# Pooling head and router of an expert-choice MoE encoder: rows spread by the tensor engine, constants loaded later, projection ahead of pooling, router on unnormed rows

## The chip, the cores and the metric

One core of one Trainium2 chip. The metric is the device time of one execution in microseconds (us), the median of several. The engines are PE (matmul), DVE (vector), ACT (scalar), POOL (GpSimd) and SP (which only issues DMAs here). Each engine runs its own list of instructions in order; they are tied together by semaphores, which one engine raises and another waits for.

## The reference, cut to what matters

2048 rows of x and 16 meta rows ahead of them make T = 2064 rows of D = 1024. Depth is 1, so there is one pooling mixer and one mixture of experts.

```python
h = concat([meta, x])                      # (2064, 1024)
u = rmsnorm(h, norm_mix)
for g, win in enumerate((2, 4, 8, 16)):    # 256 columns each
    p[g] = window_mean(u[g], win) - u[g]
h = h + concat(p[g] @ pool_w[g]) * pool_scale
u = rmsnorm(h, norm_ffn)
aff = softmax(u @ router_w)                # 16 experts
g, idx = top_k(aff.T, 258)                 # each expert picks 258 rows
ys = (silu(u[idx] @ w_gate) * (u[idx] @ w_up)) @ w_down * g
h = h.at[idx].add(ys)
out = rmsnorm(h, norm_final)[16:]
```

## The kernel before

It has three stages in one program. **Stage 1** (the head and a loop over 19 tiles, up to about 150 us) takes tiles of 128 rows that advance by 112 (eight rows of halo on either side). **Stage 2** (to about 214 us) turns the logits into affinities, finds each expert's threshold by a search in octal digits and makes the list of the first expert. **Stage 3** runs the 16 experts with split fp32 weights (a rounded high part and a rest, three products), and the final norm. The change touches stage 1 and the first lines of stage 2.

What happens to tile t in stage 1, with the engine and the line of the profile in brackets:

- SP loads `h_in` (L521; four buffers, so tile t+4 is asked for when tile t is `mixed`).
- `square_in`: ACT squares and sums each row (L839) and takes the root (L827).
- `make_band`: DVE inverts it (L1077) and scales the pooling matrix with it into `band` (L1081). There are three kinds of pooling matrix: kind 0 for the first tile, 1 for the middle ones, 2 for the last.
- PE pools: 8 fp32 matmuls of 128 columns, 16 passes in the profile, into banks 0 and 1 (L1505, `bank<-band,h_in`).
- ACT rounds the result to `pooled_hi` (L855); DVE takes the rest, `pooled_lo` (L1099).
- PE projects: 24 matmuls of 256 columns with `pw_hi` and `pw_lo`, into banks 2 and 3.
- DVE adds `h_in` and writes `h_mid` (L1118, semaphore `mixed`); SP stores it to `h_acc` (L563).
- ACT squares `h_mid` (L864) and takes the root; DVE inverts it and writes `u_out` = h_mid x inverse x norm_ffn (L1109, semaphore `normed`); SP stores it to `u_rows` (L567).
- PE turns `u_out` (8 transposes, L1510) into banks 4 and 5; ACT copies them to `u_t` (L874).
- PE forms the logits with `rw_wide` (16 passes of 32 weight columns), DVE copies them to `partial` (L1095), and one more matmul with the constant `fold` puts the tile's 16 logits per row into bank 6 (semaphore `routed`).

The work is software pipelined. "Step i" of an engine holds, in this order, on PE: pooling of tile i+1, logits of tile i-3, projection of tile i, fold of tile i-3, turning of tile i-2. On DVE: band of i+2, partial of i-3, pooled_lo of i+1, u_out of i-1, h_mid of i. On ACT: pooled_hi of i+1, square_in of i+2 (in the written-out steps before the loop `square_in` comes first), square of h_mid i-1, u_t of i-2. Steps -1 to 2 are written out (`FIRST = 3`), then a loop of 3 turns with 4 steps each, then the last steps are written out, up to step NT + 2 = 21. The steps above NT are the tail, where PE turns rows first.

Before step 0 the weights of the projection are made: `scale_weights(i)` on DVE multiplies one half of `pool_w` by norm_mix (a column per partition, `nmix`, turned by PE from `nmix_rows`) and by pool_scale (`pscale`, the row copied to all 128 partitions by DMA), 4 instructions for a half (L1134); ACT rounds the half to `pw_hi` (L880); DVE takes the rest, `pw_lo` (L1143). SP issues every load of the head in one list: the meta rows, tile 0, kind 0, the identity, the norm row, tile 1, kind 1, `pscale`, both halves of `pool_w`, tile 2, `nffn`, `rw`, kind 2, tile 3, then `chunk_quad`, `far`, `reset`, the other constants and `nfin`. The last eight that count for `loaded_c` are waited for together by POOL, DVE and PE.

After step 21 DVE waits for all 19 folds and starts the softmax: the maximum (L1174), the subtraction (L1175), and ACT the exponential (L891).

## Time and profile before

| | us |
|---|---|
| median of 3 runs | 2455.67 |
| lowest and highest run | 2455.53, 2458.54 |
| the profiled execution's own time | 2459.78 |
| its span from first to last instruction | 2457.9 |
| PE busy in it | 2386.1 (97%) |
| DVE, ACT, POOL busy | 1865.9, 1204.1, 844.8 |
| mean granted PE clock | 0.984 of full |

The profile is of one execution. Its own time lies 4.1 us above the median of the timed runs, and its span lacks 1.9 us of it, which is start and end outside the first and last instruction. A timeline row gives the start, the length (for a group, from first start to last end), the engine, the line, the operation with output and inputs, the count, and in brackets how long the engine had been idle before it and what released it. A PE matmul in fp32 appears as two passes.

### The profile page before, as it was taken

How to read it: one execution, taken by the hardware profiler on the slowest of the kernel's cores; microseconds unless marked ns; L12 is line 12 of the kernel's file. 1: busy time of each engine (PE TensorE's matmuls, PEld its weight loads, DVE VectorE, ACT ScalarE, POOL GpSimd, SP SyncE). 2: the span in 40 equal slices, each digit the busy share in tenths (PEclk: the TensorE clock that was granted, in tenths of full speed). 3: DMA queues.
4: the chain of work that ended last, by engine and by line, in shares of the span. 5: the costliest groups of instructions: out<-in, count | busy, mean ns of one | idle time of the engine just before them, and what ended most of it. 6: DMA issues, size and time to landing. Idle time of an engine off the chain costs nothing.

```text
span 2457.9 us, 48606 instructions
## 1 busy us (share of the span) xinstructions
PE 2386.1 (97%) x17338; PEld 2228.5 (91%) x17338; DVE 1865.9 (76%) x2259; ACT 1204.1 (49%) x1938; POOL 844.8 (34%) x1013
## 2 busy tenths in 40 slices
PE   7958999999999999999999999999999999999997
PEld 7947989898999989899998989899998989899996
DVE  5666786869787786968788686968778686968765
ACT  5754444444544444454444444454444444454564
POOL 0001525234251524334251524335152533425111
PEclk9978999999999999999999999999999999999998
DMA  7764648486775858586774858586674948576594
GB/s 236 215 195 131 186 133 257 150 243 184 210 201 157 228 144 252 158 238 173 207 213 141 242 141 249 157 238 188 184 216 136 250 143 250 170 228 199 161 335 171
DMA packets 345810, 486.11 MB, mean 198 GB/s; under 512 B 23117, under 2 KB 294997, under 8 KB 345778
## 3 DMA queue, kind: packets, MB, share of 16 engines
q1 hardware_dynamic: 318370, 433.82, 59.2%
q0 software_dynamic: 23232, 36.67, 7.0%
q10 hardware_dynamic: 4176, 15.21, 1.6%
q8 instruction: 18, 0.29, 0.0%
q14 instruction: 14, 0.11, 0.0%
HBM read 443.27 MB, written 46.31 MB: 199 GB/s over the span
## 4 chain that ended last, share of the span: by engine, by line
PE 87%; issue 3%; DVE 1%; POOL 1%; ACT 1%; DMA 0%; DVEq 0%; POOLq 0%; ACTq 0%
PE bank L1505 86%; PE bank L1510 1%; ACT marks_a L913 0%; POOL fin L788 0%; DMA x_rows<-u_rows,idx 0%; DVE w_lo L1345 0%; POOL h_rows L796 0%; DVE h_rows L1466 0%; POOL fin L784 0%; POOL out L817 0%; DVE x_lo L1350 0%; DVE key_t L1226 0%; DVE y_rows L1457 0%; DVE marks_v L1200 0%; DVE flag L1207 0%
## 5 line engine op out<-in xcount | busy, mean ns | idle before, releaser
L1505 PE MATMUL bank<-x_lo,w_hi 128*128 128x258 f32 x4096 | 1157.6, 283 | 0.0
L1505 PE MATMUL bank<-x_hi,w_hi 128*128 128x258 f32 x4096 | 1156.5, 282 | 0.8 <-DVE w_lo L1345 0.7
L1505 PE MATMUL bank<-x_hi,w_lo 128*128 128x258 f32 x4096 | 1155.9, 282 | 0.0
L1345 DVE TENSOR_TENSOR w_lo<-raw,w_hi 128x1024 fp32r<-128x1024 f32 x584 | 713.8, 1223 | 114.0 <-ACT w_hi L935 109.7
L1505 PEld LDWEIGHTS bank<-x_hi,w_hi 128*128 128x128 f32 x4096 | 776.1, 189 | 14.7 <-issue 13.0
L1505 PEld LDWEIGHTS bank<-x_hi,w_lo 128*128 128x128 f32 x4096 | 777.6, 190 | 0.0
L1505 PEld LDWEIGHTS bank<-x_lo,w_hi 128*128 128x128 f32 x4096 | 776.9, 190 | 0.6
L935 ACT ACTIVATE w_hi<-raw 128x1024 fp32r<-128x1024 f32 x581 | 612.2, 1054 | 312.0 <-PE bank L1505 295.2
L671 POOL TENSOR_TENSOR carrier<-carrier 128x1 f32<-128x1 f32 x360 | 115.3, 320 | 1125.7 <-ACT y_rows L986 454.8
L716 POOL DMA_INDIRECT list_rows<-pair_now,slot_now x285 | 410.1, 1439 | 137.1 <-issue 137.1
L1371 DVE SCALAR_TENSOR_TENSOR acc_left<-raw,hid_left,acc_left 128x1024 f32<-128x1024 f32 x330 | 422.5, 1280 | 0.0
L1404 DVE TENSOR_TENSOR hid<-silu,bank 128x258 f32<-128x258 f32 x256 | 108.1, 422 | 329.4 <-PE bank L1505 329.4
L1505 PE MATMUL bank<-w_hi,hid_hi 128*128 128x512 f32 x960 | 304.5, 398 | 0.0
L1505 PE MATMUL bank<-w_lo,hid_hi 128*128 128x512 f32 x960 | 299.7, 393 | 0.0
L1505 PE MATMUL bank<-w_hi,hid_lo 128*128 128x512 f32 x960 | 299.2, 393 | 0.0
L1003 ACT ACTIVATE hid_left<-hid 128x2 f32<-128x2 f32 x244 | 49.7, 204 | 435.2 <-DVE hid L1404 435.2
L1345 DVE TENSOR_TENSOR w_lo<-raw_more,w_hi 128x1024 fp32r<-128x1024 f32 x184 | 224.8, 1222 | 40.2 <-ACT w_hi L935 38.4
L935 ACT ACTIVATE w_hi<-raw_more 128x1024 fp32r<-128x1024 f32 x184 | 193.7, 1053 | 101.8 <-PE bank L1505 101.8
L998 ACT ACTIVATE silu<-bank 128x258 f32<-128x258 f32 x256 | 99.0, 387 | 280.9 <-PE bank L1505 280.9
L1505 PEld LDWEIGHTS bank<-w_hi,hid_lo 128*128 128x128 f32 x960 | 180.6, 188 | 41.4
L1505 PEld LDWEIGHTS bank<-w_lo,hid_hi 128*128 128x128 f32 x960 | 180.4, 188 | 41.2
L1505 PEld LDWEIGHTS bank<-w_hi,hid_hi 128*128 128x128 f32 x960 | 175.1, 188 | 35.5
(209 smaller groups left out, 1887.9 us busy)
## 6 DMA issues: line engine op xcount, KB each, us to landing
raw<-in_moe_w_down SPq DMA_DIRECT2D x98, 1024.0 KB
raw<-in_moe_w_gate SPq DMA_DIRECT2D x97, 1024.0 KB
raw<-in_moe_w_up SPq DMA_DIRECT2D x97, 1024.0 KB
raw_more<-in_moe_w_gate SPq DMA_DIRECT2D x31, 1024.0 KB
raw_more<-in_moe_w_up SPq DMA_DIRECT2D x31, 1024.0 KB, 8.5
raw_more<-in_moe_w_down SPq DMA_DIRECT2D x30, 1024.0 KB, 6.5
h_in<-in_x SPq DMA_DIRECT2D x18, 512.0 KB, 5.6
h_acc<-h_mid SPq DMA_DIRECT2D x17, 448.0 KB, 4.9
```

The costliest lines, as they stand in the source:

```text
L671: nc.gpsimd.tensor_tensor(carrier[:, 0:1], carrier[:, 1:2], carrier[:, 1:2], ALU.mult)\
L716: pool.indirect_dma_start(list_rows, bass.IndirectOffsetOnAxis(ap=slot_now[:, c:c + 1], axis=0), pair_now[:, c, :], None, bounds_check=CAP ...
L935: nc.scalar.activation(w_hi[:, a % 4], split_view(a, last), ACT.Copy).then_inc(split_hi, 1)
L998: nc.scalar.activation(silu[:, fc], bank[:, q % 4, 0:CAP], ACT.Silu)\
L1003: nc.scalar.activation(hid_left[:, 4 * b + fc], hid[:, fc % 2, 256:CAP], ACT.Copy)\
L1345: nc.vector.tensor_tensor(w_lo[:, a % 4], split_view(a, last), w_hi[:, a % 4].bitcast(f32), ALU.subtract).then_inc(split_lo, 1)
L1371: nc.vector.scalar_tensor_tensor(out=acc_left[:, t], in0=down_row_view(k), scalar=by, in1=acc_left[:, t], op0=ALU.mult, op1=ALU.add)\
L1404: nc.vector.tensor_tensor(hid[:, fc % 2], silu[:, fc], bank[:, q % 4, 0:CAP], ALU.mult).then_inc(hid_done, 1)
L1505: return nc.tensor.matmul(dst, lhs, rhs, start=start, stop=stop)
L1510: return nc.tensor.matmul(dst, src, ident[0:n, 0:n], is_transpose=True, start=True, stop=True)
```

## The change

- `pscale` and `nffn` are no longer loaded as a row copied to 128 partitions (512 KB each). ACT issues four small loads at its start, ahead of its table load: the 8 rows of norm_mix and of norm_ffn into `nmix_rows` (now 16 rows), and the row of pool_scale and of norm_ffn, each into one partition of `h_mid`. PE spreads each with two matmuls of 512 columns, weights `ones` of one row (`spread_row`): pool_scale into banks 2 and 3, where `scale_weights` reads it, norm_ffn into banks 4 and 5, from where ACT copies it to `nffn`.
- PE runs `square_ones(6)` (6 matmuls of 128 columns that nothing reads) before the first spread and `square_ones(12)` after the second.
- SP loads `pool_w` before tile 1 and kind 1. Kind 2, `chunk_quad`, `far`, `reset` and `nfin` (five loads) are issued by `load_late`, after `tile_out(0)` and `tile_out(1)`, ahead of `tile_out(2)`.
- In DVE's head, tile 1's band moves behind the making of the weights. On ACT, `square_in` of tile 1 moves behind both `pw_hi`, and in step 0 `square_in` of tile 2 now comes after `pooled_hi` of tile 1 (`early` is 0 < i0 < FIRST).
- On PE, in step 0 the pooling of tile 1 comes after the projection of tile 0 (`pool_rows`).
- The router works on `h_mid`: PE turns `h_mid` instead of `u_out`, a step earlier (tile i-1 at the end of step i, logits and fold of i-2 in step i). norm_ffn goes into `rw_wide` (POOL), and the inverse root mean square is applied to all logits at once in stage 2: `rms2` keeps all 19 columns, a reciprocal and one more multiplication by `inv_all` come ahead of the maximum. PE's and DVE's last step is NT + 1 instead of NT + 2, ACT's NT instead of NT + 1.

The diff, cut:

```diff
@@ SP, the head's loads
             load_kind(0, loaded_kind0)
-            sp.dma_start(ident[:], ...).then_inc(loaded_nmix, 16)
-            sp.dma_start(nmix_rows[:], norm_mix[0].rearrange("(k p) -> k p", p=P)).then_inc(loaded_nmix, 16)
-            load_tile(1, 1)
-            load_kind(1, loaded_kind1)
-            sp.dma_start(pscale[:], pool_scale[0].partition_broadcast(P)).then_inc(loaded_pw[0], 16)
+            sp.dma_start(ident[:], ...).then_inc(loaded_ident, 16)
             for i in range(2):
                 ...
                 sp.dma_start(pw[:, half], pool_w_v[:, half]).then_inc(loaded_pw[i], 16)
+            load_tile(1, 1)
+            load_kind(1, loaded_kind1)
             load_tile(2, 2)
-            sp.dma_start(nffn[:], norm_ffn[0].partition_broadcast(P)).then_inc(loaded_c, 16)
             sp.dma_start(rw[:], ...).then_inc(loaded_c, 16)
-            load_kind(2, loaded_c)
             load_tile(3, 3)
-            (chunk_quad, far, reset: three loads)
             sp.dma_start(cst[:, POOL_COLS:], consts[:, POOL_COLS:]).then_inc(loaded_c, 16)
-            sp.dma_start(nfin[:], norm_final.partition_broadcast(P)).then_inc(loaded_c, 16)
+            def load_late():
+                (kind 2, chunk_quad, far, reset, nfin: five loads, each .then_inc(loaded_late, 16))
...
             for i in range(FIRST - 1):
                 tile_out(i, 0, load_tile)
+            load_late()
@@ POOL
-            nc.gpsimd.tensor_copy(rw_wide[:, :, 0:NE], rw[:]).then_inc(rw_widened, 1)
+            pool.wait_ge(nmix_out, 1)
+            nffn_across = nmix[:, KD:2 * KD].unsqueeze(2).broadcast_to([P, KD, NE])
+            nc.gpsimd.tensor_tensor(rw_wide[:, :, 0:NE], rw[:], nffn_across, ALU.mult).then_inc(rw_widened, 1)
@@ ACT
+            for i, rows in enumerate((norm_mix, norm_ffn)):
+                nc.scalar.dma_start(nmix_rows[KD * i:KD * (i + 1), :], rows[0].rearrange("(k p) -> k p", p=P))\
+                  .then_inc(loaded_nmix, 16)
+            for i, row in enumerate((pool_scale, norm_ffn)):
+                nc.scalar.dma_start(h_mid[0:1, i, :], row).then_inc(loaded_rows[i], 16)
             nc.scalar.preload_act_table(ACT.Sqrt)
...
-                early = isinstance(j, int) and i0 < FIRST
+                early = isinstance(j, int) and 0 < i0 < FIRST
...
             square_in(-1, 0, 1)
-            step(-1, 0)
+            act.wait_ge(pooled, 1)
+            nc.scalar.activation(pooled_hi[:, 0, :], two_banks(0), ACT.Copy).then_inc(pooled_hi_done, 1)
             for k in range(0, KD, 4):
                 act.wait_ge(weights_scaled, k + 4)
                 nc.scalar.activation(pw_hi[:, k:k + 4], pw[:, k:k + 4], ACT.Copy).then_inc(weights_hi, 1)
+            square_in(0, 0, 1)
+            act.wait_ge(nffn_spread, 1)
+            nc.scalar.activation(nffn[:], two_banks(4), ACT.Copy).then_inc(nffn_out, 1)
@@ DVE, the head
-            dve.wait_ge(loaded_kind1, 16)
-            make_band(0, 0, 1)
+            dve.wait_ge(scale_spread, 1)
...
             scale_weights(0)
             step(-1, 0, banded_before=True)
             scale_weights(1)
-            (pw_lo of both halves)
+            split_weights(0)
+            split_weights(1)
+            dve.wait_ge(loaded_kind1, 16)
+            make_band(0, 0, 1)
@@ DVE, the start of stage 2
+            dve.wait_ge(rooted2, NT)
+            link(nc.vector.reciprocal(inv_all[:], rms2[:]))
             dve.wait_ge(routed, NT)
-            link(nc.vector.tensor_reduce(peak[:], logits, AX.X, ALU.max))
-            nc.vector.tensor_tensor(lg[:], logits, over_experts(peak[:]), ALU.subtract).then_inc(shifted, 1)
+            link(nc.vector.tensor_tensor(lg[:], logits, over_experts(inv_all[:]), ALU.mult))
+            link(nc.vector.tensor_reduce(peak[:], lg[:], AX.X, ALU.max))
+            nc.vector.tensor_tensor(lg[:], lg[:], over_experts(peak[:]), ALU.subtract).then_inc(shifted, 1)
@@ PE
             def turn_rows(i0, j):
-                s = (i0 - 2) % 2
-                pe.wait_ge(normed, upto(i0, j, -2))
+                s = (i0 - 1) % 2
+                pe.wait_ge(mixed, upto(i0, j, -1))
                 ...
-                                      u_out[:, s, k * P:(k + 1) * P])
+                                      h_mid[:, s, k * P:(k + 1) * P])
...
+            def square_ones(times):
+                for _ in range(times):
+                    mm(bank[:, 6, 0:P], ones[:], ones[:], True, True)
+
+            def spread_row(i, done):
+                pe.wait_ge(loaded_rows[i], 16)
+                for half in range(2):
+                    last = mm(bank[:, 2 + 2 * i + half, :], ones[0:1, :],
+                              h_mid[0:1, i, half * 512:half * 512 + 512], True, True)
+                last.then_inc(done, 1)
+
+            pe.wait_ge(setup_p, 1)
+            square_ones(6)
+            spread_row(0, scale_spread)
+            pe.wait_ge(loaded_ident, 16)
             pe.wait_ge(loaded_nmix, 32)
-            turn_block(bank[:, 7, 0:KD], nmix_rows[:]).then_inc(nmix_turned, 1)
+            turn_block(bank[:, 7, 0:2 * KD], nmix_rows[:]).then_inc(nmix_turned, 1)
             for i in range(-1, FIRST):
                 ...
                 step(i, 0)
+                if i == -1:
+                    spread_row(1, nffn_spread)
+                    square_ones(12)
...
-            for i in range(FIRST + BODY * TURNS, NT + 3):
+            for i in range(FIRST + BODY * TURNS, NT + 2):
                 step(i, 0)
```

## Rows read from the trace of the kernel before

**Rows 1.** The page, section 1: span, then busy time of each engine.
```profile
span 2457.9 us, 48606 instructions
PE 2386.1 (97%) x17338; PEld 2228.5 (91%) x17338; DVE 1865.9 (76%) x2259; ACT 1204.1 (49%) x1938; POOL 844.8 (34%) x1013
```
**Rows 2.** The chain that ended last, one piece: start, length, what.
```profile
333.12 129.15 PE bank L1505 x932
```
**Rows 3.** Timeline of all engines, 0 to 20 us: start, length, engine, line, operation.
```profile
6.75 0.49 DVE L1081 TENSOR_SCALAR band<-cst,inv 128x512 f32<-128x512 f32 x1
7.29 3.47 PE L1505 MATMUL bank<-band,h_in 128*128 128x128 f32 x16 [1.10 <-DVE band L1081]
10.80 1.02 ACT L855 ACTIVATE pooled_hi<-bank 128x1024 fp32r<-128x1024 f32 x1 [2.10 <-PE bank L1505]
11.71 1.67 DVE L1134 SCALAR_TENSOR_TENSOR pw<-pw,nmix,pscale 128x256 f32<-128x256 f32 x4 [2.19 <-DMA pw<-in_pool_w]
12.84 2.03 SPq L546 DMA_DIRECT2D chunk_quad<-in_consts  x1
13.30 1.22 DVE L1099 TENSOR_TENSOR pooled_lo<-bank,pooled_hi 128x1024 fp32r<-128x1024 f32 x1
14.66 3.75 PE L1505 MATMUL bank<-band,h_in 128*128 128x128 f32 x16 [3.90 <-DVE pooled_lo L1099]
16.01 2.43 DVE L1143 TENSOR_TENSOR pw_lo<-pw,pw_hi 128x1024 fp32r<-128x1024 f32 x2
17.09 1.04 ACT L839 ACTIVATE squares<-h_in 128x1024 f32<-128x1024 f32 x1
18.25 0.29 ACT L827 ACTIVATE rms<-ss,eps 128x1 f32<-128x1 f32 x1
18.50 0.58 PE L1505 MATMUL bank<-pw_hi,pooled_hi 128*128 128x256 f32 x1
```
**Rows 4.** Slices of 1 us: busy PE, PEld, DVE, ACT, POOL; granted clock; DMA share; GB/s.
```profile
13.00:14.00 1.00, 0.00 (x0) 0.00 (x0) 1.00 (x2) 0.59 (x1) 0.00 (x0) 0.85 1.01 410
20.00:21.00 1.00, 1.00 (x8) 1.00 (x8) 0.73 (x1) 0.97 (x3) 0.00 (x0) 0.74 0.72 276
```
**Rows 5.** Timeline of all engines, 20 to 45 us.
```profile
24.18 0.38 SPq L521 DMA_DIRECT2D h_in<-in_x  x1
30.88 1.06 ACT L839 ACTIVATE squares<-h_in 128x1024 f32<-128x1024 f32 x1 [4.19 <-DMA h_in<-in_x]
38.05 0.38 SPq L521 DMA_DIRECT2D h_in<-in_x  x1
44.51 1.05 ACT L839 ACTIVATE squares<-h_in 128x1024 f32<-128x1024 f32 x1
```
**Rows 6.** Timeline of PE alone, 36.5 to 49 us.
```profile
37.34 0.38 PE L1505 MATMUL bank<-pw_hi,pooled_hi 128*128 128x256 f32 x1
40.57 1.07 PE L1510 MATMUL bank<-ident,u_out 128*128 128x128 f32 x8
41.48 2.00 PE L1505 MATMUL bank<-band,h_in 128*128 128x128 f32 x16
48.18 0.90 PE L1505 MATMUL bank<-band,h_in 128*128 128x128 f32 x6
```
**Rows 7.** DMA issues, 0 to 60 us: count, KB each, median us to landing.
```profile
h_in<-in_x SPq DMA_DIRECT2D x9, 512.0 KB, 5.8
nfin<-in_norm_final SPq DMA_DIRECT2D x1, 512.0 KB, 6.5
```
**Rows 8.** Timeline of all engines, 139 to 152 us.
```profile
139.71 1.23 DVE L1118 TENSOR_TENSOR h_mid<-bank,h_in 128x1024 f32<-128x1024 f32 x1 [0.86 <-PE bank L1505]
144.45 1.02 ACT L874 ACTIVATE u_t<-bank 128x1024 f32<-128x1024 f32 x1
150.23 0.61 PE L1505 MATMUL bank<-cst,partial 128*128 128x16 f32 x2 [0.41 <-DVE partial L1095]
151.46 0.47 DVE L1175 TENSOR_TENSOR lg<-bank,peak 128x304 f32<-128x304 f32 x1
```

More of the change, by code:

```diff
@@ L187, in encoder_kernel @@
         far = sb("far", [P, 1], f32)
+        rms2 = sb("rms2", [P, NT], f32)
+        inv_all = sb("inv_all", [P, NT], f32)
         listed = sb("listed", [P, 3, 5], f32)
@@ L509, in upto, with column @@
             return i0 + a + 1 + BODY * j
+        def column(i0, j, a):
+            return slice(i0 + a, i0 + a + 1) if isinstance(j, int) else ds(i0 + a + BODY * j, 1)
         def turn(i0, j, a, ring):
@@ L1134, in scale_weights, with split_weights @@
                     nc.vector.scalar_tensor_tensor(out=pw[:, k, :], in0=pw[:, k, :], scalar=nmix[:, k:k + 1],
-                                                   in1=pscale[:, g * GD:(g + 1) * GD], op0=ALU.mult,
+                                                   in1=two_banks(2)[:, g * GD:(g + 1) * GD], op0=ALU.mult,
                                                    op1=ALU.mult).then_inc(weights_scaled, 1)
+            def split_weights(i):
+                half = slice(4 * i, 4 * i + 4)
+                dve.wait_ge(weights_hi, i + 1)
+                nc.vector.tensor_tensor(pw_lo[:, half], pw[:, half], pw_hi[:, half].bitcast(f32),
+                                        ALU.subtract).then_inc(pw_split, 1)
             scale_weights(0)
@@ L1527, in step @@
                 tail = isinstance(j, int) and i0 >= NT
[L1528 removed]
+                if tail and here(-1):
                     turn_rows(i0, j)
[L1530 to L1543 removed]
+                if here(1) and not (isinstance(j, int) and i0 == 0):
+                    pool_rows(i0, j)
+                if here(-2):
+                    pe.wait_ge(turned_out, upto(i0, j, -2))
+                    s = (i0 - 2) % 2
+                    if i0 == 2:
                         pe.wait_ge(rw_widened, 2)
[L1545 to L1546 removed]
+                    if upto(i0, 0, -4) > 0:
+                        pe.wait_ge(part_out, upto(i0, j, -4))
                     for k in range(KD):
```

124 lines of the change are left out of this document (64 added, 60 removed).

## The prediction

> **What bounds the kernel now.** I read the page first: PE is busy 97% of a span of 2457.9 us [rows 1]. The chain of waits shows where: from 214 us on it is PE in long pieces, such as 129.15 us without a break in one expert [rows 2]. No line of the experts changes, so nothing is to be had or lost there, and everything from the softmax to 214 us is a chain of short waits that the change moves as a whole but for one multiplication. So the question is only at what time the softmax starts: the last fold ends at 150.84 and the subtraction at 151.93 [rows 8]. I then read the timeline up to 152 us, and the slices of 1 us for the clock. The loop over tiles is bound by PE too: pooling of one tile at 41.48, of the next at 48.18, 6.70 us a step with the turning, projection and logits between them and no idle time [rows 6]. What does not lie on PE's time there is hidden, and what stops PE there is lost for good. So two places carry the sum: the head, until PE runs without breaks, and the tail, from the last `h_mid` on.
>
> **The change part by part.**
>
> The head before, for comparison: pooling of tile 0 takes 7.29 to 10.76, the weights arrive at 11.71, `pw_lo` is ready at 18.44, the projection starts at 18.50, and pooling of tile 1 has filled the wait (14.66 to 18.41) [rows 3]. The first projection that starts in a full step is tile 3's, at 37.34 [rows 6]. That is the mark against which I walk through the head after. All steps below are start plus duration, in the order of each engine's list.
>
> Loads. Two copies of 512 KB leave the head, and `pool_w` goes ahead of tile 1 and kind 1: some 1.3 MB instead of 2.6 MB lie ahead of its first half's end. The half landed at 11.71 [rows 3]; at the roughly 0.3 MB per us that the DMA engines move in full slices (410 and 276 GB/s [rows 4]) it lands near 7.4, the second half near 9. The row of pool_scale is issued by ACT as its third load, at some 1.6 us; no row shows such a load, so it lands between 3.5 and 6; I take 4.2, since no large transfer is ahead of it on its queue.
>
> PE's new work. 8 fp32 matmuls of 128 columns (1024 columns) took 3.47 us at the start [rows 3] and 2.00 us in the loop [rows 6]: the pace of the 1.2 and of the 2.4 GHz level. (The slices call the clock 1.00 before 13 us, but the pace is that of the low level.) `square_ones(6)` is 768 columns, 2.6 us at the low level, 1.1 to 3.7. `spread_row` is 1024 columns with one row of weights. I charge it like a pooling, 3.47 us at the low level: 4.2 to 7.7. This holds the queue: the turn of the norm rows and the pooling of tile 0, which started at 7.29, wait behind it, and so does `scale_weights(0)`, which needs the spread. The rule that speaks against this edit is in the Trainium skill, "TensorE: Matmul & The Clock Gate", section "Why this matters for your kernels": a matmul with few rows of weights takes the same time as one with 128. By it the spread costs what I charge; were it cheaper in proportion to its rows, pooling of tile 0 could start at 7.3 and the sum would be 0.6 us lower. No row here shows a one-row matmul of this width.
>
> The clock. A busy PE got the high level within slice 20:21, about 6 us after it had begun at 14.66, and had lost it in slice 13:14, about 3 us after its work had ended at 10.76 [rows 3, 4]. Busy from 1.1 on, with half a us of gap, it would have the high level near 7.1. So I let the pooling of tile 0 run at the high level: 7.9 to 9.9. If it stays low, it ends 1.5 us later.
>
> Weights. `pooled_hi` 1.02 gives 10.9, `pooled_lo` 1.22 gives 12.1; `scale_weights(0)` (1.67) was done at 9.7 between nmix and this. `scale_weights(1)` 1.67 gives 13.8; `pw_hi` about as long as `pooled_hi`, 14.9; `split_weights`, 2.43 for both from 13.8, gives 16.2 [rows 3]. The projection of tile 0 starts at 16.2 instead of 18.5 and at the high level, 2.8 us (37.34 to about 40.2, ahead of the fold and the turn at 40.57 [rows 6]): ends 19.0.
>
> Projection ahead of pooling. Now nothing has been pooled in the wait. Pooling of tile 1 runs 19.0 to 21.0. Then comes a chain with PE idle: `pooled_hi` to 22.0; **ACT squares tile 2 only behind it**, since step 0 is no longer early (from 17.09 to the root's end at 18.54 it took 1.45 [rows 3]), to 23.5; DVE's list has the band of tile 2 ahead of `pooled_lo` of tile 1, so inverse and band (0.7) to 24.2, `pooled_lo` to 25.4, and only then pooling of tile 2, 25.4 to 27.4. `h_mid` of tile 0 is behind `pooled_lo`: 26.6. This 4.4 us of idle PE is new. In the loop the same chain exists but a projection, a fold and a turn hide it; here they are already over or not yet there. From then on: projection of tile 1 to 30.2, turning of tile 0 (1.07) to 31.3, and steps of 6.70: pooling of tile 3 at 31.3, of tile 4 at 38.0, projection of tile 3 at 40.6 (37.34 came 2.7 after its pooling). Tile 4's load is issued at 27 and takes 6.7 (24.18 to 30.88 before [rows 5]), so it lands at 33.7, and its square, `pooled_hi`, `pooled_lo` (4 us) end at 37.6, just in time. **Head: 40.6 - 37.3 = +3.3 us.** In it are the 1.9 us of logits, fold and turn of one tile which the new order does one step earlier; they come back in the tail.
>
> Late constants. `load_late` starts after the store of `u_out` 1, near 39.5, and puts five issues (0.4 each, 2.0 where a column load was slow [rows 3]) and some 0.92 MB ahead of the store of `h_mid` 2 and of the load of tile 6. That load normally has 44.51 - 38.05 = 6.46 us from issue to need and lands in 5.8 [rows 5, 7]: 0.7 us of slack. Issued 1 us late behind 0.92 MB (3 us) it is up to 3.3 us late; but the engines are not full all the time. Behind the square on DVE's list are the band and `pooled_lo`, and PE's next pooling waits for these with no slack. Bounds 0 and 3.3; I take **+1.8**. Before, these loads cost nothing: they stood in the head, and what waited for them (POOL, and PE at step 2) was not late. The new waits on them cost nothing: POOL's stands ahead of its work for stage 2 (from 156 us), DVE's ahead of the band of tile 18, both some 70 us after the loads.
>
> Router on unnormed rows. In the loop the counts are the same and each item keeps its place in the step, so the loop stays at 6.70. `rw_wide` by a multiplication instead of a copy on POOL and the reciprocal of 19 columns are hidden behind the tiles. In the tail, with `h_mid` of tile 18 done at 140.94 [rows 8] as before: turning of tile 17 is at the end of step 18 already, tile 18's turn comes when `u_t` of 17 is out, 141.9 to 143.0, ACT copies it in the slot at 144.45 (squares, root and the table load of the exponential are ahead of it on ACT) to 145.47 [rows 8]; logits 0.65, partial 0.3 and fold 0.4 with their hand-overs end at 146.95 instead of 150.84. That is 3.9 us; the multiplication by `inv_all` costs like the subtraction, 0.47 plus its wait, 0.5. **Tail: -3.4.**
>
> Sum: +3.3 + 1.8 - 3.4 = **+1.7 us**. Against the profiled execution 2459.78 that is 2461.5; that execution stands 4.1 us above the median, so the median should go from 2455.67 to **2457.4**.
>
> **The rivals.**
>
> A, the clock (slower). The one mechanism is PE's clock in the head. The new gap of 4.4 us (21.0 to 25.4) is longer than the 3.9 us ahead of 14.66 in which the high level was lost. If it is lost, PE runs at 1.2 GHz for some 5 to 6 us from 25.4, and does 2.6 us less work. If it also comes late, tile 0's pooling and with it all to 16.2 is 1.5 us later. Both: +4.1, total +5.8: 2461.5. It decides where PE stands idle as long as in the one gap that lost it, 3.9 us; my 4.4 is only just beyond that. Against it: the dummy matmuls keep PE busy up to some 14.4, and it isn't known that a gap always costs the level.
>
> B, the chain is not exposed (faster). If tile 2 is squared or `pooled_lo` ready in time, so that the 4.4 us idle do not arise, and the late loads find room: 1.7 - 4.4 - 1.8 = -4.5, 2451.2; with a spread that is cheap, 2450.6. Against it stands the plain order of ACT's and DVE's lists.
>
> C, the late loads are harmless, the rest as forecast: -0.1, 2455.6.
>
> D, the tail doesn't gain: if ACT's table load and squares delay `u_t` in a new way or DVE's list holds the last partial behind the last `u_out`, the gain shrinks to 1 or 2 us: 2459.
>
> **How the numbers follow.** Forecast 0.42, A 0.17, B 0.14, C 0.17, D 0.10. A measurement of this kernel can tell about 0.2%, 4.9 us, from no change; that is, below 2450.8 or above 2460.6. Half of A and more lies above, with a part of D: slower 0.15. B and what I may have overcharged (rows at 3.5 us, slack in DMA) lie partly below: faster 0.13. Same 0.72. Range: 2451.0 to 2461.8 holds all but the ends of A and B.
>
> **What would show it.** In the timeline after: the projection of tile 0 starting near 16 to 18 rather than 18.5; pooling of tile 1 behind it; PE idle for some 4.4 us released by `pooled_lo`; ACT idle on the load of tile 6 at about 48 us with an idle PE of 1 to 2 us after it; the slice of the clock between 24 and 30 at 1.00 (for A: 0.50); the projection of tile 3 near 40.6; only two groups of logits after the last `h_mid` instead of three, and the subtraction ending some 7.7 us after `h_mid`'s end instead of 11. I am wrong if the loop's step isn't 6.70, or if the first expert starts earlier than 214 us by more than 3.

## The result, and the profile after

The changed kernel is slower by about 7 us.

| | before | after |
|---|---|---|
| median of 10 runs each, us | 2457.14 | 2464.05 |
| lowest and highest, us | 2455.53, 2460.32 | 2461.37, 2464.89 |
| ratio, 95% interval | | 1.0027 [1.0020, 1.0035] |
| the profiled execution's own time | 2459.78 | 2464.18 |

The forecast was 2457.4, range 2451.0 to 2461.8: the time lies above the range. Of the 6.7 us that were missed, 1.5 is that the median of before is 2457.14 over ten runs and was 2455.67 over three. The rest, 5.2, is the change itself: +6.9 where I had +1.7.

The page of after, section 1: span, then the busy time of each engine.

```profile
span 2462.4 us, 48730 instructions
PE 2396.0 (97%) x17382; PEld 2235.9 (91%) x17382; DVE 1866.8 (76%) x2261; ACT 1205.6 (49%) x1939; POOL 853.0 (35%) x1013
```

Beside [rows 1] PE is busy 9.9 us longer. 44 more matmul passes are no loss by themselves; the question is which of them hold up others. The experts are as they were, so, as before, I read the timeline up to 157 us. First the head of after, of all engines, with the rows that make the chain up to the third pooling.

```profile
1.14 2.93 PE L1541 MATMUL bank<-ones 128*128 128x128 f32 x12 [1.14 <-POOL ones L660]
...
1.69 0.27 ACTq L849 DMA_DIRECT2D h_mid<-in_pool_scale  x1
...
4.86 3.78 PE L1541 MATMUL bank<-h_mid,ones 1*128 1x512 f32 x4 [0.80 <-DMA h_mid<-in_pool_scale]
5.73 1.06 ACT L860 ACTIVATE squares<-h_in 128x1024 f32<-128x1024 f32 x1 [2.15 <-DMA h_in<-in_x]
...
8.60 3.58 PE L1541 MATMUL bank<-band,h_in 128*128 128x128 f32 x16
...
12.11 1.98 PE L1541 MATMUL bank<-h_mid,ones 1*128 1x512 f32 x4
12.21 1.02 ACT L899 ACTIVATE pooled_hi<-bank 128x1024 fp32r<-128x1024 f32 x1 [5.01 <-PE bank L1541]
...
14.02 4.41 PE L1541 MATMUL bank<-ones 128*128 128x128 f32 x24
14.41 1.65 DVE L1160 SCALAR_TENSOR_TENSOR pw<-pw,nmix,bank 128x256 f32<-128x256 f32 x4
...
15.98 2.66 DVE L1168 TENSOR_TENSOR pw_lo<-pw,pw_hi 128x1024 fp32r<-128x1024 f32 x2
...
18.79 0.36 PE L1541 MATMUL bank<-pw_hi,pooled_hi 128*128 128x256 f32 x1 [0.36 <-DVE pw_lo L1168]
```

The weights landed earlier, by 8.92 at the latest, when DVE starts to scale the first half (11.71 in [rows 3]), and it did not help: the first projection starts at 18.79, and before it started at 18.50 [rows 3]. The pooling of tile 0 starts 1.3 us later than before and takes 3.58 us, which is nearly the pace of the low level, and behind it the same chain `pooled_hi`, `pooled_lo`, second half of the weights, `pw_lo` runs as before.

The next stretch of the same view has the new order.

```profile
21.69 1.95 PE L1541 MATMUL bank<-band,h_in 128*128 128x128 f32 x16
...
23.68 1.02 ACT L876 ACTIVATE pooled_hi<-bank 128x1024 fp32r<-128x1024 f32 x1 [4.25 <-PE bank L1541]
24.60 1.05 ACT L860 ACTIVATE squares<-h_in 128x1024 f32<-128x1024 f32 x1
...
26.29 0.49 DVE L1108 TENSOR_SCALAR band<-cst,inv 128x512 f32<-128x512 f32 x1
26.70 1.22 DVE L1126 TENSOR_TENSOR pooled_lo<-bank,pooled_hi 128x1024 fp32r<-128x1024 f32 x1
...
28.06 3.00 PE L1541 MATMUL bank<-band,h_in 128*128 128x128 f32 x16 [4.42 <-DVE pooled_lo L1126]
```

The number in brackets is how long PE stood idle: 4.42 us, released by `pooled_lo`, because ACT squares tile 2 only behind `pooled_hi` and DVE has the band ahead of `pooled_lo`. The pooling behind the gap takes 3.00 us, and the one ahead of it took 1.95. The slices of after (engine columns as in [rows 4], then the granted clock, DMA share and GB/s) say why.

```profile
24.00:25.00 1.00, 0.00 (x0) 0.00 (x0) 0.00 (x0) 1.00 (x2) 0.00 (x0) 1.00 0.00 0
...
29.00:30.00 1.00, 1.00 (x6) 1.00 (x6) 0.60 (x3) 0.00 (x0) 0.00 (x0) 0.50 0.14 37
```

At 24 PE is idle and the clock is still 1.00; at 29 it is 0.50, the 1.2 GHz level. In slice 32:33 it comes back.

Last, the tail of after.

```profile
147.64 1.23 DVE L1145 TENSOR_TENSOR h_mid<-bank,h_in 128x1024 f32<-128x1024 f32 x1 [0.89 <-PE bank L1541]
...
152.39 1.02 ACT L895 ACTIVATE u_t<-bank 128x1024 f32<-128x1024 f32 x1
...
154.53 0.40 PE L1541 MATMUL bank<-cst,partial 128*128 128x16 f32 x2 [0.41 <-DVE partial L1122]
...
155.03 0.47 DVE L1209 TENSOR_TENSOR lg<-bank,inv_all 128x304 f32<-128x304 f32 x1
...
156.04 0.47 DVE L1211 TENSOR_TENSOR lg<-lg,peak 128x304 f32<-128x304 f32 x1
```

From the last `h_mid` to the subtraction it is 8.40 us; it was 11.75 in [rows 8]. The tail gained what it should. But `h_mid` itself starts at 147.64 instead of 139.71.

One execution of before was not enough to compare with. I took two more traces of it and a second one of after (after_again), and the marks are these (starts in us, each one row of its timeline; the mean is of the three of before):

| | before | before_again | before_third | mean | after | after_again |
|---|---|---|---|---|---|---|
| first projection, tile 0 | 18.50 | 19.20 | 18.58 | 18.76 | 18.79 | 21.15 |
| projection of tile 1 | 24.02 | 23.82 | 23.32 | 23.72 | 30.71 | 33.43 |
| projection of tile 3 | 37.34 | 36.14 | 35.06 | 36.18 | 44.08 | 46.46 |
| last `h_mid` | 139.71 | 138.52 | 137.57 | 138.60 | 147.64 | 150.45 |
| subtraction | 151.46 | 150.60 | 148.39 | 150.15 | 156.04 | 159.06 |
| first product of the first expert | 207.10 | 205.45 | 203.66 | 205.40 | 211.61 | 214.39 |

after_again took 2467.26 us, more than any of the ten timed runs, and 2.4 of its 3.0 us above after are there at the first projection. The first trace of after, at 2464.18, stands close to the median, so I use it. With it the ledger is: up to the projection of tile 1 +7.0, to that of tile 3 +0.9, to the last `h_mid` +1.1, the tail -3.15, to the first expert +0.3, the rest of the span +1.1; sum +7.3 of span, where the medians say +6.9.

### The profile page after: what moved, and what is told of

It is laid out like the page before. It is cut to its first block, busy times and chain, and to the rows that moved or that the text cites. A ratio compares the mean times of both kernels' runs of the same rounds, so it can differ in the third digit from the quotient of the medians.

```text
span 2462.4 us, 48730 instructions
## 1 busy us (share of the span) xinstructions
PE 2396.0 (97%) x17382; PEld 2235.9 (91%) x17382; DVE 1866.8 (76%) x2261; ACT 1205.6 (49%) x1939; POOL 853.0 (35%) x1013
## 3 DMA queue, kind: packets, MB, share of 16 engines
HBM read 442.23 MB, written 46.31 MB: 198 GB/s over the span
## 4 chain that ended last, share of the span: by engine, by line
PE 87%; issue 3%; DVE 1%; POOL 1%; ACT 1%; DMA 0%; DVEq 0%; POOLq 0%; ACTq 0%
PE bank L1541 86%; PE bank L1546 1%; ACT marks_a L938 0%; POOL fin L804 0%; DMA x_rows<-u_rows,idx 0%; DVE w_lo L1381 0%; POOL h_rows L812 0%; DVE h_rows L1502 0%; POOL fin L800 0%; POOL out L833 0%; DVE x_lo L1386 0%; DVE key_t L1262 0%; DVE y_rows L1493 0%; DVE marks_v L1236 0%; DVE flag L1243 0%
## 5 line engine op out<-in xcount | busy, mean ns | idle before, releaser
L1541 PEld LDWEIGHTS bank<-x_hi,w_hi 128*128 128x128 f32 x4096 | 776.4, 190 | 14.4 <-issue 13.0
```

The costliest lines, as they stand in the source:

```text
L1541: return nc.tensor.matmul(dst, lhs, rhs, start=start, stop=stop)
```

## The experiments

All timed kernels in one table; the difference is to the median of before, timed beside it on the same chip.

| kernel | median us | runs | difference | ratio, 95% interval |
|---|---|---|---|---|
| after | 2464.05 | 10 | +6.9 | 1.0027 [1.0020, 1.0035] |
| b_router | 2455.47 | 11 | -1.2 | 0.9995 [0.9986, 1.0004] |
| a_early | 2462.26 | 11 | +5.6 | 1.0020 [1.0011, 1.0029] |
| a_late_head | 2463.91 | 9 | +7.2 | 1.0026 [1.0016, 1.0036] |
| a_fill_gap | 2462.78 | 11 | +6.1 | 1.0023 [1.0014, 1.0032] |
| a_pool_first | 2458.16 | 11 | +1.9 | 1.0007 [0.9998, 1.0016] |
| a_no_ones | 2466.59 | 5 | +10.4 | 1.0041 [1.0027, 1.0055] |
| a_pf_late | 2456.98 | 11 | -0.3 | 0.9996 [0.9987, 1.0005] |
| b_shift | 2456.97 | 11 | -0.3 | 0.9999 [0.9990, 1.0008] |
| a_rows128 | 2467.07 | 5 | +9.8 | 1.0035 [1.0021, 1.0048] |
| b_best | 2455.95 | 11 | -1.4 | 0.9992 [0.9983, 1.0001] |

Four more executions were taken for their traces alone: before_again (2456.27 us), before_third (2454.78), after_again (2467.26) and rows128_again, the kernel of a_rows128 (2464.91); before took 2456.86 beside the last two.

My theory at the outset: the head's new order costs most (the exposed chain, and the clock lost in it), the late constants about 1 us, the router part gains. The rivals: the router part costs time itself; the gap alone counts and not the clock; the spread and the dummy matmuls are what makes the head late.

### The router part alone

b_router is the kernel before with only the router's part of the change.

```diff
-                s = (i0 - 2) % 2
-                pe.wait_ge(normed, upto(i0, j, -2))
+                s = (i0 - 1) % 2
+                pe.wait_ge(mixed, upto(i0, j, -1))
...
-                                      u_out[:, s, k * P:(k + 1) * P])
+                                      h_mid[:, s, k * P:(k + 1) * P])
...
+            link(nc.vector.tensor_tensor(lg[:], logits, over_experts(inv_all[:]), ALU.mult))
```

> The kernel before with the router's part of the change alone (PE turns h_mid a step earlier, norm_ffn in rw_wide, inverse rms on all logits at once; both norm rows loaded by SP). Theory 1 (the tail gains, the head loses): from the end of the last h_mid to the end of the subtraction 7.6 us instead of 11.0, the loop's step stays 6.70, the whole 3.4 us faster than before, ratio 0.9986. Rival R (the router's part is what costs, for instance in the loop): the step is longer than 6.70, or the time is at or above before, ratio 1.000 or more.

Measured -1.2 us where 3.4 were expected, with an interval that includes no change and just reaches the 3.4. In its trace the last `h_mid` starts at 140.09 (before, mean of three: 138.60), the subtraction at 148.48 (150.15), the first expert's first product at 203.69 (205.40). So the tail gives what it gives in after, 8.39 us instead of 11.55, and 1.5 us of it are lost earlier. Of these, 0.7 are there at the first projection (19.43; 18.76), where nothing of the router's order has run yet: the weights landed at 12.64 instead of 11.71 [rows 3], and one more load, the rows of norm_ffn, stands ahead of theirs in SP's list. That this load is the cause isn't shown; they landed at 12.41 in before_again. Another 0.4 is a slower first stretch (5.41 us from the projection of tile 0 to that of tile 1, mean of before 4.96), and 0.3 lie between the projections of tiles 1 and 3 (12.78; mean 12.46), where logits, fold and turn of one tile come a step earlier than before. The loop is as it was: 102.5 us from the projection of tile 3 to the last `h_mid`, before 102.4. So the router's part is a small gain in this trace, 1.7 us at the first expert, and not shown by the times. The slowdown of after isn't here.

### Where ACT squares tile 2

a_early lets ACT square tile 2 ahead of `pooled_hi` in step 0 again.

```diff
-                early = isinstance(j, int) and 0 < i0 < FIRST
+                early = isinstance(j, int) and i0 < FIRST
```

> The changed kernel, but ACT squares tile 2 ahead of pooled_hi of tile 1 in step 0 again. Theory 1 (the idle PE behind the pooling of tile 1 is a chain through ACT's square of tile 2): the gap goes from 4.42 to about 2.3 us, PE keeps its clock in it, so 2.1 us and up to 1.8 us more are saved: 2 to 4 us less than the changed kernel. Rival L (tile 2 lands too late for that, so that its square would hold up pooled_hi): the gap stays at 4.4 us or grows.

PE alone, a_early, from the second spread to the pooling behind the gap:

```profile
16.13 5.00 PE L1541 MATMUL bank<-ones 128*128 128x128 f32 x24
20.89 0.37 PE L1541 MATMUL bank<-pw_hi,pooled_hi 128*128 128x256 f32 x1
...
28.18 2.02 PE L1541 MATMUL bank<-band,h_in 128*128 128x128 f32 x16 [2.46 <-DVE pooled_lo L1126]
```

The gap is 2.46 us instead of 4.42, and the pooling behind it runs at full pace, 2.02 instead of 3.00: the square was 2 us of the gap, and the clock was lost with a gap of 4.42 and kept with one of 2.46. From the projection of tile 0 to that of tile 3 it is 21.71 us instead of 25.29 (25.31 in after_again), 3.6 less. The times give only 1.3, with intervals that overlap. In the traced execution 2.1 of the 3.6 are lost at once: the second spread and the dummy matmuls ran at the low level until past 20 and held the projection of tile 0 to 20.89. That happens in after too (21.15 in its second trace), and how often in each kernel one or two traces can't tell; so the size of this gain stays open between 1.3 and 3.6.

### The gap filled

a_fill_gap is after with dummy matmuls in the gap, so that the wait stays and the clock doesn't fall.

```diff
                         pool_rows(i0, j)
+                        square_ones(16)
```

> The changed kernel with 16 more matmuls of ones behind the pooling of tile 1 in step 0, 3.9 us of PE work in the idle 4.42 us. It removes no wait. Theory 1 (part of the loss is the clock lost in that gap): the granted clock stays 1.00 from 24 to 34 us, pooling of tile 2 takes 1.95 instead of 3.00 us, and 1.5 to 2 us are saved. Rival N (the clock falls anyway, or its loss is hidden behind ACT and DVE): less than 0.5 us is saved.

PE alone, a_fill_gap:

```profile
22.85 3.74 PE L1541 MATMUL bank<-ones 128*128 128x128 f32 x32
27.43 2.02 PE L1541 MATMUL bank<-band,h_in 128*128 128x128 f32 x16 [0.85 <-DVE pooled_lo L1126]
```

The pooling keeps its pace. From its start to the projection of tile 3 (41.84) it is 14.41 us, in after 16.02 (28.06 to 44.08). So the fallen clock costs 1.6 us; the times, +6.1 against +6.9, show half of it, with intervals that allow the whole. The wait itself, still 4.4 us between the two poolings, is the larger term.

The same trace shows that the length of a gap alone doesn't decide. Here the first spread ran at the high level (1.99 us at 4.45), PE then stood idle for 1.69 us, until 8.13, for the load of the identity, and the clock fell at about 8.0:

```profile
7.00:8.00 1.00, 0.00 (x0) 0.00 (x0) 0.58 (x2) 0.27 (x1) 0.00 (x0) 0.96 0.96 332
8.00:9.00 1.00, 0.87 (x4) 0.84 (x5) 0.24 (x2) 0.00 (x0) 0.00 (x0) 0.50 1.08 415
```

So it was lost with a shorter gap than the 2.46 us with which a_early kept it; what stood ahead of the gap was a one-row spread here, and a projection and a pooling there.

### Pooling ahead of the projection again

a_pool_first undoes the reordering on top of a_early: tile 1 is squared, banded and pooled ahead of the projection of tile 0, as before; loads, spreads and router stay as in after.

```diff
             square_in(-1, 0, 1)
+            square_in(0, 0, 1)
...
             scale_weights(0)
...
+            dve.wait_ge(loaded_kind1, 16)
+            make_band(0, 0, 1)
...
-                if here(1) and not (isinstance(j, int) and i0 == 0):
+                if here(1):
...
-                    if isinstance(j, int) and i0 == 0:
-                        pool_rows(i0, j)
...
-                    square_ones(12)
```

> The changed kernel with the order of the head undone: PE pools tile 1 ahead of the projection of tile 0, the band of tile 1 is made behind scale_weights(0), ACT squares tiles 1 and 2 early, and the 12 matmuls of ones behind the second spread are gone, as the pooling takes their place. Spreads, loads, late constants and router as changed. Theory 1 (the loss is the order): the projection of tile 0 starts near 18.7 as in the changed kernel, pooling of tile 2 follows near 22 instead of 28, and the subtraction ends 5 to 6 us earlier: 2457 to 2459 or less. Rival P (the loss is the spreads and the loads, which the order only shows): the time stays within 1.5 us of the changed kernel.

Measured +1.9 instead of +6.9: 5.0 us of the slowdown hang on this order, the early square of tile 2 and the second group of dummy matmuls, which went with it. The projection of tile 1 starts at 24.76 (before 23.72, after 30.71). From there to the last `h_mid` the trace has 1.7 us more than before, 1.4 of them in the step with the late loads (below); then the tail gives 3.15 back, and the subtraction, at 149.73, is level with before (150.15).

### The late constants

a_late_head is after with the five late loads issued at the end of the head's list; a_pf_late is a_pool_first with the same edit.

```diff
+            load_late()
+
...
-            load_late()
```

> The changed kernel, but the five late loads are issued right behind the head's other loads, where the DMA engines were idle from 15 to 29 us. Theory 1: the load of tile 6 is issued in time, the step of 7.67 us at 48.4 becomes 6.70, and 0.97 us are saved. Rival D (the loads do more harm in the head, by delaying tile 4 or the stores): a wait for tile 3 or 4 appears and the time does not fall.

> The kernel with the order of the head undone (PE pools tile 1 first, tile 2 squared early, no second group of ones) and also the late loads moved back into the head: of the whole change only the spreads, the first ones, pool_w ahead of tile 1 and the router remain. Theory 1 (order and late loads are the two losses): the stretched step of 8.07 us at 41.7 becomes 6.70 and the time falls 1.4 us below the kernel with the order undone, to 2456 or 2457. Rival P (something of the spreads still costs): it stays at 2458 or above.

After, all engines, where the late loads stand (SPq rows are DMA issues), in a window cut at 57 us; then PE in a_late_head in windows cut at 49 and 57 us. So some counts and lengths are parts; the starts are whole.

```profile
41.97 1.43 SPq L540 DMA_DIRECT2D cst<-in_consts  x1
...
44.89 0.44 SPq L563 DMA_DIRECT2D nfin<-in_norm_final  x1
...
46.31 0.36 SPq L533 DMA_DIRECT2D h_in<-in_x  x1
...
48.42 2.00 PE L1541 MATMUL bank<-band,h_in 128*128 128x128 f32 x16
...
52.41 1.06 ACT L860 ACTIVATE squares<-h_in 128x1024 f32<-128x1024 f32 x1 [0.84 <-DMA h_in<-in_x]
...
56.09 1.12 PE L1541 MATMUL bank<-band,h_in 128*128 128x128 f32 x8
```

```profile
48.56 0.66 PE L1542 MATMUL bank<-band,h_in 128*128 128x128 f32 x4
...
55.27 1.90 PE L1542 MATMUL bank<-band,h_in 128*128 128x128 f32 x15
```

From pooling to pooling that step takes 7.67 us in after instead of 6.70, since ACT had to wait for the tile. In a_late_head it takes 6.71 (55.27 - 48.56): the 0.97 us are gone. In a_pool_first the step with the loads took 8.07 (41.73 to 49.80), in a_pf_late 6.70. The medians show nothing for a_late_head, +7.2 against +6.9, where the interval is as wide as the effect, and -2.2 us for a_pf_late against a_pool_first. The step's length is the better witness: 1.0 us in after, 1.4 in a_pool_first, and between 0.7 (a_rows128, 7.39) and 1.4 (after_again, 8.09) in all traces with the late loads. With both edits the kernel is back at the time of before, -0.3.

### The dummy matmuls

a_no_ones is after without either group of dummy matmuls.

```diff
-            square_ones(6)
...
-                    square_ones(12)
```

> The changed kernel without both groups of ones matmuls (6 ahead of the first spread, 12 behind the second). They feed nothing. Theory 1 (they buy little: the pooling of tile 0 ran at the low level all the same, and when the clock is low the 12 hold up the projection): the time stays within 1 us, or is lower in executions where the clock is low behind the second spread. Rival W (they keep the clock up): the projection of tile 0 runs at the low level (3.7 instead of 2.9 us) and the time rises by about 1 us or more.

Its median is 3.5 us further above before than that of after, as the rival had it and not as I had; with five runs the intervals still overlap. Its slices:

```profile
20.00:22.00 2.00, 2.00 (x12) 2.00 (x11) 0.00 (x0) 0.00 (x0) 0.00 (x0) 0.50 0.00 0
```

The projection of tile 0 starts at the same time, 18.86, and runs at the low level; the pooling of tile 1 starts at 23.47 instead of 21.69, and the last `h_mid` is 2.0 us later. So in this trace of after the dummy matmuls, which end at 18.43, don't hold the head up, and they save 1.8 us of slow projection: they run low themselves, but the clock is back when the projection starts. In after_again they do hold it up:

```profile
12.79 3.78 PE L1541 MATMUL bank<-h_mid,ones 1*128 1x512 f32 x4
16.50 4.89 PE L1541 MATMUL bank<-ones 128*128 128x128 f32 x24
21.15 0.36 PE L1541 MATMUL bank<-pw_hi,pooled_hi 128*128 128x256 f32 x1
```

`pw_lo` was ready there at 19.22 and the projection started 1.9 us later, behind them; in a_early, where the second spread ran low too, it was 2.0. So the dummy matmuls save time in one kind of execution and cost as much in another, and the medians, +10.4 against +6.9, speak for keeping them without being clear of noise.

### One row of weights, or 128

Why do they run low at all? a_rows128 is after with `h_mid` zeroed first and the spreads made with all 128 rows of `ones`, which sum the same values.

```diff
+            for i in range(2):
+                nc.vector.memset(h_mid[:, i, :], 0.0).then_inc(rows_zeroed, 1)
...
-                    last = mm(bank[:, 2 + 2 * i + half, :], ones[0:1, :],
-                              h_mid[0:1, i, half * 512:half * 512 + 512], True, True)
+                    last = mm(bank[:, 2 + 2 * i + half, :], ones[:],
+                              h_mid[:, i, half * 512:half * 512 + 512], True, True)
```

> The changed kernel, but the two spreads use 128 rows of weights instead of one: DVE sets h_mid to zero first, the row lands in partition 0, and the sum over 128 rows is the same row. Same columns, same output, 0.4 us later at most. Theory K (PE work with one row does not hold or raise the granted clock, so that the clock is lost or comes late behind the spreads): with 128 rows the pooling of tile 0 or at the latest the second spread runs at the high level, the 12 ones take 2.9 us instead of 4.4 to 5, and the time falls by up to 1 us. Rival N (rows do not matter to the clock): the same low stretches as in the changed kernel.

> The changed kernel, unchanged, for a second trace. Theory K: the 12 ones behind the one-row spread take 4.4 to 5.0 us again, and the clock is lost again in the idle stretch before the pooling of tile 2. Rival N: one of the two runs at the high level throughout.

> The changed kernel with spreads of 128 rows of weights once more, for a second trace. Theory K: as in the first one, the second spread (1.9 us) and the 12 ones behind it (2.8 us) run at the high level. Rival N (the first trace was chance): the ones take 4.4 us or more, as in the four traces with one-row spreads.

PE alone, a_rows128:

```profile
6.89 2.80 PE L1545 MATMUL bank<-h_mid,ones 128*128 128x512 f32 x4 [2.83 <-DMA h_mid<-in_pool_scale]
...
12.43 1.88 PE L1545 MATMUL bank<-h_mid,ones 128*128 128x512 f32 x4
14.15 2.84 PE L1545 MATMUL bank<-ones 128*128 128x128 f32 x24
```

The slices of a_rows128 and, in the second fence, of after:

```profile
14.00:16.00 2.00, 2.00 (x18) 1.85 (x17) 2.00 (x4) 0.60 (x1) 0.00 (x0) 1.00 0.40 161
```

```profile
16.00:18.00 2.00, 2.00 (x11) 2.00 (x10) 2.00 (x3) 1.90 (x2) 2.00 (x3) 0.50 0.00 0
```

Behind a spread with one row the twelve dummy matmuls took 4.41 us (after), 5.00 (a_early), 4.47 (a_late_head), 4.52 (a_fill_gap) and 4.89 (after_again); behind one with 128 rows 2.84 in both traces. In after, a_late_head and a_fill_gap the clock had been high during the spread and fell behind it while PE was busy; in a_early and after_again it was low from before. So in all seven traces what stands ahead of the dummy matmuls, one row or 128, goes with the level at which they run; why the chip does this the runs don't say. It gave no time here: the row landed at 6.89 and 7.12, two us later than in after, since ACT's load, issued at 1.69 in after, now waited for DVE's zeroes until 3.03, and the second half of the weights and the gap of 4.42 us stayed, with 3.60 us of pooling behind it. The kernel stands at +9.8, its interval overlaps that of after, and the spans of its two traces, 2463.8 and 2463.1, lie between after's 2462.4 and 2465.4. As a theory of the clock behind the second spread it holds. That the one-row spreads cost time in the median isn't shown: the late row hides what the higher level would give.

The width is one more thing to read here: at the high level the one-row spread took 1.98 us (after, at 12.11), the 128-row one 1.88. The rule weighed in the prediction (the Trainium skill, "TensorE: Matmul & The Clock Gate", section "Why this matters for your kernels": few rows of weights take the time of 128) agrees with this.

### Other traces, other addresses

before_again and before_third are the kernel before once more. The last stage, from the last long piece of the experts to the end, was 174.3 us in the first trace of before, 172.45 and 172.73 in these, and 173.6 to 175.8 in the kernels with the router's part. A router change also shifts every later buffer by 152 bytes. b_shift is before with that shift and nothing else.

```diff
+        spare1 = sb("spare1", [P, NT], f32)
+        spare2 = sb("spare2", [P, NT], f32)
```

> The kernel before, unchanged, for a second trace. Its profiled execution was 4.1 us above its median. Theory S (that execution was a slow one in its head or tail, as the clock happened to fall; the typical one starts the experts some 2 us earlier than 214.3 us): a trace near the median of 2456 to 2457 shows the first expert's products near 212 us and a different granted clock before 21 us or between 142 and 152 us. Rival E (the scatter lies in the experts): the first products stay near 214.3 and the stretch from there to the end differs.

> The same once more, for a third trace: what differs between executions of one kernel, and by how much. Theories as for the second trace.

> The kernel before with nothing changed but two unused tensors of 76 bytes per partition in the place where the change puts rms2 and inv_all, so that every later buffer lies 152 bytes higher. Up to now 2 of 3 traces of before need 172.6 us from the last expert's second gate block to the end, and all 7 traces of kernels with the router's part 174.2 to 175.2. Theory A (the addresses cost it): the stretch is 174 us or more and the time 1.5 to 2 us above before. Rival S (chance of the DMAs in the last stage, or something else in the router's part): the time is that of before within 1 us.

b_shift takes the time of before, -0.3, and an interval of [-2.5, +2.0] us. No cost of the addresses is shown. Its last stage took 175.2 us in the trace, as theory A had it, but its time is that of before; so this stage differs by 2 or 3 us between executions of kernels that take the same time. The 1.1 us that the ledger has there are not shown to belong to the change. Why only two traces of before are under 173 us stays open.

The traces of before also show where the first one was late. All engines, before_third, then before_again: the square of tile 4, which stood at 30.88 in [rows 5]. Its load was issued at 23.48, 23.98 and, in the first trace, 24.18, so it was there 5.1, 5.7 and 6.7 us after its issue.

```profile
28.60 1.06 ACT L839 ACTIVATE squares<-h_in 128x1024 f32<-128x1024 f32 x1 [2.61 <-DMA h_in<-in_x]
```

```profile
29.68 1.06 ACT L839 ACTIVATE squares<-h_in 128x1024 f32<-128x1024 f32 x1 [3.19 <-DMA h_in<-in_x]
```

### A version meant to beat both

b_best is b_router with `pool_w` loaded ahead of tile 1, both halves of the weights scaled ahead of `pooled_lo`, and eight dummy matmuls behind the first pooling.

```diff
-            load_tile(1, 1)
-            load_kind(1, loaded_kind1)
...
+            load_tile(1, 1)
+            load_kind(1, loaded_kind1)
...
-            dve.wait_ge(loaded_kind1, 16)
-            make_band(0, 0, 1)
...
             scale_weights(0)
+            scale_weights(1)
...
+                if k == 4:
+                    dve.wait_ge(loaded_kind1, 16)
+                    make_band(0, 0, 1)
...
+                    for _ in range(8):
+                        mm(bank[:, 6, 0:P], ones[:], ones[:], True, True)
```

> The kernel before with the router's part, pool_scale and pool_w loaded ahead of tile 1 and kind 1 (as copied rows, no spread), scale_weights of both halves ahead of pooled_lo of tile 0, and 8 matmuls of ones between the poolings of tile 0 and 1. PE's order stays: pooling of tile 1 ahead of the projection of tile 0. If DVE's queue in the head is what sets the start of the projection: it starts near 17.1 instead of 18.5 to 19.4 and the kernel is 1 to 2 us faster than the one with the router's part alone, 2453.5 to 2454.5. Rival: tile 1, now later, holds up its pooling, and nothing is gained.

All engines, b_best:

```profile
14.66 1.21 DVE L1156 TENSOR_TENSOR pw_lo<-pw,pw_hi 128x1024 fp32r<-128x1024 f32 x1
...
15.99 0.49 DVE L1094 TENSOR_SCALAR band<-cst,inv 128x512 f32<-128x512 f32 x1
...
16.53 2.83 PE L1521 MATMUL bank<-band,h_in 128*128 128x128 f32 x16 [3.91 <-DVE band L1094]
19.00 0.56 PE L1521 MATMUL bank<-pw_hi,pooled_hi 128*128 128x256 f32 x1
```

The weights landed at 10.36, and DVE's order took what that gave: PE stood idle 3.91 us for the band of tile 1, which DVE makes only behind `pooled_lo` and the first half of `pw_lo`, and the projection started at 19.00, no earlier than in before. The later load of tile 1 was not what held it, as the rival had it: ACT squared tile 1 at 13.02, without a wait. Its median is 1.4 us below before's, the interval reaches 1.0001. Neither this kernel nor b_router is shown to beat the kernel before.

## Why the prediction was wrong, point by point

**The change in the head: +3.3 forecast, +7.9 found.** Three steps carry the 4.6 us.

- *"The projection of tile 0 starts at 16.2"*: it started at 18.79, 2.6 us later. The row of pool_scale came at 4.86 (taken 4.2), the spread ended at 8.6 (taken 7.7), and the pooling of tile 0 started at 8.60 (taken 7.9): 0.7 us. Tile 0's square was late too (5.73; 4.97 before), but its band was ready at 8.00, before the spread ended. Then *"I let the pooling of tile 0 run at the high level"*: it took 3.58 us, not 2.0, 1.6 us. I had reasoned that a PE busy from 1.1 on gets the level near 7.1. It didn't by 8.60, nor by the pace of this pooling before about 12. Why stays open. a_rows128 doesn't settle it: its pooling took 2.76 (2.47 in rows128_again), but started 1.2 and 2.5 us later, and by the paces the level rose at about 11.3 and 12.1, no earlier than in after. The price, "if it stays low, it ends 1.5 us later", was right, and stood in rival A only. The last 0.3 us are in the weights behind it: from the start of `scale_weights(1)` to the projection 4.4 us (14.41 to 18.79), where the walk had 4.1.
- *The clock in the gap*: rival A said that 4.4 us idle lose the level and 2.6 us with it. It was lost, but from 28.9 to 32.3 only, not for 5 to 6 us, and a_fill_gap prices it at 1.6. My own walk had been 0.8 too dear in the same stretch (15.2 us from that pooling to the projection of tile 3, where 14.41 is what it takes at full pace, since the first steps are 6.2 and 6.4 us long and not 6.70), so that 0.8 shows. Both halves of A's mechanism happened, at 1.6 each instead of 1.5 and 2.6.
- *The mark of comparison, 37.34*: it is of one execution in which tile 4's load landed late (30.88, and 28.60 and 29.68 in the two others). The same mark is 36.14 and 35.06 there, so the mean is 1.2 us earlier. I had measured the head after, in which such a wait is hidden behind the gap, against a head before in which it was exposed.

2.6 + 0.8 + 1.2 = 4.6. Medians don't show these terms one by one; the traces carry them, and all are of the first trace of after. In after_again the projection of tile 0 started 2.4 us later still, 1.9 of them because the dummy matmuls at the low level held it up, a cost that the prediction had put at nothing ("the dummy matmuls keep PE busy up to some 14.4"; they ended at 18.43 and 21.39).

**The exposed chain was right.** "4.4 us of idle PE", released by `pooled_lo`, was 4.42, step by step as walked through. Its parts held too: 2 of it are the square of tile 2 (a_early). a_pool_first shows that 5.0 of the 6.9 us go with this order. The sum had expected that the earlier start of the projection (-2.3) pays for half of it, and it never came earlier.

**Late constants: +1.8 forecast, +1.0 found** (7.67 instead of 6.70 for that step). The step named, ACT waiting for tile 6's load, was right, and 0.84 us of ACT's idle time is in the row at 52.41. The bound of 3.3 assumed DMA engines that were full; the tile took 6.1 us from its issue at 46.31, hardly more than the 5.8 of [rows 7], so that only the lateness of the issue counted. That was 2.6 us against a_late_head (43.73), not the 1 us of the walk, and the slack took most of it.

**Tail: -3.4 forecast, -3.15 found** (11.55 to 8.40). Right, with the order of events as told. The loop's step was 6.70. That the router's step earlier costs 1.9 in the head was taken too high: b_router lost 0.3 there, and 1.0 against before_third alone (12.78 to 11.74), in which PE didn't wait for tile 4.

**The rest**: +0.3 to the first expert and +1.1 behind, which the scatter of the last stage can be.

In sum 3.3 + 4.6 for the head, 1.8 - 0.8, -3.4 + 0.25, and 1.4 for the rest (with 0.2 of rounding in the loop) make the +7.3 of the ledger. A, at 0.17 the second likeliest with C, had been priced at 2461.5 beside a base that was 1.5 too low and a mark 1.2 too late.

## What to carry to other kernels

When one group of matmuls is moved ahead of another, ask first what the other one had hidden. Here the projection came no earlier, and the pooling that had filled the wait for the weights was missed at once, since its own chain (round, rest, square, band) then had nothing to stand behind. When a mark of one trace is the base of a difference of 1 or 2 us, take a second trace of the same kernel; a load that lands late in one of them is 1 us. And a term that is only a rival's, such as the clock at the start, should be in the forecast when nothing in the trace shows the better case.

## What the runs showed of the hardware

- Matmuls with one row of weights went with a low clock behind them. Twelve dummy matmuls behind a one-row spread took 4.41 to 5.00 us in five traces, behind a 128-row one 2.84 in both. In after the second spread ran high (1.98 us at 12.11), and the level fell in the slice from 15, at 0.62, while PE was busy without a break.
- The same dummy matmuls at the start left different levels: the first spread behind them ran at the high level in a_fill_gap (1.99 us at 4.45) and at the low one in after (3.78 us at 4.86).
- Gaps and the clock: behind 4.42 us of idle PE the pooling took 2.94 to 3.60 us in all six traces with that gap, behind 3.91 (b_best) 2.83, behind 2.46 (a_early) 2.02. But length alone doesn't tell: in a_fill_gap the level fell at about 8.0 with 1.69 us of idle PE behind the one-row spread (granted clock 0.96 in slice 7:8, 0.50 in 8:9).
- The load of one row of 4 KB, issued by ACT at 1.69, was there at 4.86: 3.2 us. In the other traces with this load and this issue it came at 4.45 to 5.35.
- A load of 512 KB took 6.7, 5.1 and 5.7 us from its issue in three traces of one kernel (tile 4, there at 30.88, 28.60 and 29.68).
